# Two transformer blocks on one core: the weight sums of the fast downward products move from SBUF to DRAM

## The reference, cut to what matters

```python
# block 1
f = (jax.nn.silu(h @ w_gate[l]) * (h @ w_up[l])) @ w_down[l]
...
# block 2
def conv_gated_mlp(h, w_up, conv_w, conv_b, w_down):
...
    return (jax.nn.silu(gate) * val) @ w_down
```

## Time and profile before

| | us |
|---|---|
| median of 3 runs | 1310.57 (1309.82 to 1311.11) |
| the profiled execution: its own time | 1310.27 |
| span from its first to its last instruction | 1308.5 |
| PE busy | 1267.4 (97%) |
| DVE, ACT, POOL busy | 966.4 (74%), 730.3 (56%), 559.4 (43%) |

### The profile page before, as it was taken

One profiled execution on the slowest core, in us unless ns is written; L12 is line 12 of the kernel. 1 busy time (PEld: TensorE's weight loads), 2 busy tenths in 40 slices (PEclk: granted clock), 3 DMA queues, 4 the chain that ended last, 5 costly groups with the idle time before them and its releaser, 6 DMA issues. The chain is left out here.

```text
span 1308.5 us, 22029 instructions
## 1 busy us (share of the span) xinstructions
PE 1267.4 (97%) x7684; PEld 1148.4 (88%) x7684; DVE 966.4 (74%) x1732; ACT 730.3 (56%) x1437; POOL 559.4 (43%) x626
## 2 busy tenths in 40 slices
PE   8999999999999977999999999999999999788998
PEld 7999988999999956889999999889899998567887
DVE  5677857899888966785565788377977777858754
ACT  5666745455555535556667788254555554445452
POOL 5655672356565543226777765310213222641000
PEclk9999999999999999999999999999999999998999
DMA  6321213343333399722212333232232323797221
GB/s 194 87 73 58 97 66 97 97 129 97 99 125 97 108 300 233 173 73 74 73 49 65 74 67 112 80 123 91 81 100 94 112 80 113 265 225 191 99 97 65
DMA packets 134855, 148.28 MB, mean 113 GB/s; under 512 B 24652, under 2 KB 110875, under 8 KB 134770
## 3 DMA queue, kind: packets, MB, share of 16 engines
q1 hardware_dynamic: 121536, 126.27, 30.4%
q0 software_dynamic: 13232, 20.89, 8.3%
q10 hardware_dynamic: 2, 0.00, 0.0%
HBM read 132.47 MB, written 2.10 MB: 103 GB/s over the span
## 5 line engine op out<-in xcount | busy, mean ns | idle before, releaser
L2836 PE MATMUL ps<-h_hi,w_hi 128*128 128x256 f32 (+1 forms) x748 | 238.4, 319 | 0.0
L2837 PE MATMUL ps<-h_lo,w_hi 128*128 128x256 f32 (+1 forms) x748 | 237.4, 317 | 0.0
L2838 PE MATMUL ps<-h_hi,w_lo 128*128 128x256 f32 (+1 forms) x748 | 237.1, 317 | 0.0
L2955 PE MATMUL ps<-w_hi,h_hi 128*128 128x384 f32 (+2 forms) x512 | 162.6, 328 | 0.0
L2957 PE MATMUL ps<-w_hi,h_lo 128*128 128x384 f32 (+2 forms) x512 | 157.9, 319 | 0.0
L2836 PEld LDWEIGHTS ps<-h_hi,w_hi 128*128 128x128 f32 x748 | 142.6, 191 | 9.6 <-DVE h_lo L2132 0.3
L2838 PEld LDWEIGHTS ps<-h_hi,w_lo 128*128 128x128 f32 x748 | 142.5, 191 | 9.6
L2837 PEld LDWEIGHTS ps<-h_lo,w_hi 128*128 128x128 f32 x748 | 142.6, 191 | 8.4
L3132 PE MATMUL ps<-w_hi,st_hi 128*128 128x512 f32 x252 | 104.5, 415 | 30.5 <-DVE w_lo L2385 18.1
L1249 POOL TENSOR_TENSOR w_lo<-w_raw,w_hi 128x384 fp32r<-128x384 f32 (+2 forms) x114 | 112.9, 1012 | 34.1 <-ACT w_hi L1512 34.1
L3133 PE MATMUL ps<-w_lo,st_hi 128*128 128x512 f32 x252 | 102.2, 405 | 0.0
(11 more groups left out here) (331 smaller groups left out, 3437.5 us busy)
## 6 DMA issues: line engine op xcount, KB each, us to landing
w_raw<-in_w_up_dram SPq DMA_DIRECT2D x25, 1024.0 KB, 5.3
w_raw<-in_w_in_dram SPq DMA_DIRECT2D x69, 256.0 KB, 3.6
w_raw<-in_w_down_dram SPq DMA_DIRECT2D x14, 1024.0 KB, 6.3
w_raw<-in_w_gate_dram SPq DMA_DIRECT2D x11, 1024.0 KB, 5.3
w_raw<-in_w_out_dram SPq DMA_DIRECT2D x8, 1024.0 KB, 5.0
h_raw<-in_w_down_dram SPq DMA_DIRECT2D x8, 1024.0 KB, 8.1
h_raw<-h_raw POOLq DMA_DIRECT2D x32, 256.0 KB, 5.3
w_raw<-in_w_up_dram SPq DMA_DIRECT2D x16, 512.0 KB, 3.8
```

The costliest lines, as they stand in the source:

```text
L2836: pe.matmul(out_, s_hi, m_hi, start=first and n == 0, stop=False, skip_group_check=True)
L2837: pe.matmul(out_, s_hi, m_lo, start=False, stop=False, skip_group_check=True)
L2838: mm = pe.matmul(out_, s_lo, m_hi, start=False, stop=last and n == len(pairs) - 1, skip_group_check=True)
L2955: pe.matmul(bank, h_hi[:, kb0 + i, tok], hi[:, i, :], start=half == 0 and i == 0, stop=False, skip_group_check=True)
```

## The change

It makes all weight sums ahead of the downward stages, in DRAM. Each block gets a DRAM tensor `down_sums[d]` with room for T1, T4, T2 and T3 of all nine pairs (256 KB each).

* SP's `sums_begin` copies, for each pair, B21 and B22 (512 KB, to T4's and T2's place) and B12 twice (256 KB each, to T1's and T3's place), DRAM to DRAM: 27 transfers a block, one pair after each projection load.
* POOL's `sums_added` issues 12 adding transfers a block, four (T3, T1, T2, T4) for each of three groups of three pairs, 768 KB each. They stand in POOL's mixer work right behind the attention units listed in ADD_AFTER. T2 = T2 + T1 waits for T1 to land (`sums_chain`), T4 waits for T2 in the same way, T3 for the copies (`sums_begun`); T1 has no wait of its own.
* The downward stages have no sums or adding transfers of weights any more. SP loads a quarter from `w_down` and three sums from `down_sums` (256 KB and 768 KB), or 512 KB and one sum of 256 KB. `down_high` on ACT waits for the loads alone. POOL issues the loads of `early_hi` together after part P4 of step 1, and those of `early_lo` together when `early_negated` allows.
* On DVE, in step 10, the block that makes `first_two` and the kept sums now stands ahead of `down_low` of B2 and `rows_added`.

```diff
-SUMMED = 4
+GROUPS = 3
+ADD_AFTER = ((9, 12, 15, 18, 20, 23, 25, 27, 29, 32, 35, 38), (8, 11, 14, 17, 20, 23, 26, 29, 32, 35, 38, 41))
+SUM_T1, SUM_T4, SUM_T2, SUM_T3 = range(4)
...
+        down_sums = [nc.dram_tensor(f"down_sums{d}", [STRASSEN, P, 4, 512], F32, kind="Internal").ap() for d in range(2)]
...
+            def group(g):
+
+                wide = STRASSEN // GROUPS
+                return slice(wide * g, wide * g + wide)
...
+                    if i < STRASSEN and j % (STRASSEN // GROUPS) == 0:
+                        sp.wait_ge(sums_ready[j // (STRASSEN // GROUPS)], 32 * d + 32)
                     if i < STRASSEN:
-                        sp.dma_start(dst.rearrange("p (k h) n -> p k (h n)", k=RB), src).then_inc(done, 16)
+                        sp.dma_start(dst[:, 0, :], src[:, 0, LEFT]).then_inc(done, 16)
+                        sp.dma_start(dst[:, 1:4, :], down_sums[d][j, :, 0:3, :]).then_inc(done, 16)
                     else:
                         sp.dma_start(dst[:, 0:2, :].rearrange("p h n -> p (h n)"), src[:, 1, :]).then_inc(done, 16)
-                        sp.dma_start(dst[:, 2, :], src[:, 0, RIGHT]).then_inc(done, 16)
+                        sp.dma_start(dst[:, 2, :], down_sums[d][j, :, SUM_T3, :]).then_inc(done, 16)
...
+            def sums_begin(d, j):
+
+
+                pair, g = slice(j, j + 1), j // (STRASSEN // GROUPS)
+                w = rows(A[("w_down", "w_down_2")[d]][0])
+                sp.dma_start(down_sums[d][j, :, SUM_T4:SUM_T2 + 1, :].rearrange("p h n -> p (h n)"), w[j][:, 1, :])\
+                    .then_inc(sums_begun[g], 16)
+                for n in (SUM_T1, SUM_T3):
+                    sp.dma_start(down_sums[d][j, :, n, :], w[j][:, 0, RIGHT]).then_inc(sums_begun[g], 16)
...
+                        normed_units += 1
+                        if normed_units in ADD_AFTER[mx.b]:
+                            n = ADD_AFTER[mx.b].index(normed_units)
+                            sums_added(mx.b, n // 4, ("T3", "T1", "T2", "T4")[n % 4])
...
+            def sums_added(d, g, name):
+
+
+                to = lambda n: down_sums[d][group(g), :, n, :]
+                from_w = lambda quarter: weight_quarter(d, group(g), quarter)
+                chain, ready = sums_chain[g], sums_ready[g]
+                if name == "T3":
+                    pool.wait_ge(sums_begun[g], 48 * (STRASSEN // GROUPS) * (d + 1))
+                    pool.dma_start(to(SUM_T3), from_w("B22"), accum_op=ALU.add).then_inc(ready, 16)
+                elif name == "T1":
+                    pool.dma_start(to(SUM_T1), from_w("B11"), accum_op=ALU.add).then_inc(chain, 16)
+                elif name == "T2":
+                    pool.wait_ge(chain, 32 * d + 16)
+                    pool.dma_start(to(SUM_T2), to(SUM_T1), accum_op=ALU.add).then_inc(chain, 16)
                 else:
-                    pool.wait_ge(down_added[n], added_at(d, i, k))
-                pool.dma_start(raw[:, dst, :], raw[:, src, :], accum_op=ALU.add).then_inc(down_added[n], 16)
-
-            def down_additions(d, i):
-
-                for n, k in ((i - 2, 2), (i - 1, 1), (i, 0)):
-                    if SUMMED <= n < STEPS and (n < STRASSEN or k == 0):
-                        down_added_to(d, n, k)
+                    pool.wait_ge(chain, 32 * d + 32)
+                    pool.dma_start(to(SUM_T4), to(SUM_T2), accum_op=ALU.add).then_inc(ready, 16)
...
             def down_high(d, i, name):
 
-                if name in ("B11", "B2"):
-                    act.wait_ge(down_raw[down_place(i)], raw_at(d, i))
-                else:
-                    sem_, value = weight_sum_ready(d, i, SUMS_OF[name])
-                    act.wait_ge(sem_, value)
+                act.wait_ge(down_raw[down_place(i)], raw_at(d, i))
```

More of the change, by code:

```diff
@@ L103, in before_in_place @@
     return earlier[-1] if earlier else None
[L106 to L117, removed]
 def weights_hi_at(d, i, k):
@@ L138, in raw_at @@
     same = [n for n in range(STEPS) if down_place(n) == down_place(i)]
-    return 16 * sum(1 if n < STRASSEN else 2 for e in range(d + 1) for n in same if e < d or n <= i)
+    return 32 * sum(1 for e in range(d + 1) for n in same if e < d or n <= i)
 def round_done(j, k=SEVEN):
@@ L833, in two_blocks_kernel @@
         down_raw = [sem(f"down_raw{n}") for n in range(6)]
-        down_added = [sem(f"down_added{n}") for n in range(6)]
-        down_sums = sem("down_sums")
+        sums_begun = [sem(f"sums_begun{n}") for n in range(GROUPS)]
+        sums_chain = [sem(f"sums_chain{n}") for n in range(GROUPS)]
+        sums_ready = [sem(f"sums_ready{n}") for n in range(GROUPS)]
         down_hi = sem("down_hi")
@@ L1022, in down_raw_of, with weight_quarter @@
             return h_raw[:, n - 2, :, :]
-        def weight_sum_ready(d, i, k):
-            return (down_sums, weight_sums_at(d, i, k)) if i < SUMMED else (down_added[down_place(i)], added_at(d, i, k))
+        def weight_quarter(d, pairs, name):
+            k, h = {"B11": (0, 0), "B12": (0, 1), "B21": (1, 0), "B22": (1, 1)}[name]
+            w = A[("w_down", "w_down_2")[d]][0].rearrange("(j k p) (h n) -> j p k h n", p=P, k=RB, n=512)
+            return w[pairs, :, k, h, :]
+        def group(g):
+            wide = STRASSEN // GROUPS
+            return slice(wide * g, wide * g + wide)
         def down_piece(w, i, name):
@@ L1175, in _ @@
             const(pool_gain[:, :], A["pool_scale"][0].rearrange("(m p) -> p m", p=P), allow_slow_non_contiguous=True)
+            begun = 0
             for n in range(2, len(mixers[0].loads)):
                 load_projection(mixers[0], n)
+                if n >= 3 and begun < STRASSEN:
+                    sums_begin(0, begun)
+                    begun += 1
+            for j in range(begun, STRASSEN):
+                sums_begin(0, j)
             out_chunks(A["w_out"][0], C_OUT1, 0)
@@ L1184, in _ @@
                     load_projection(mixers[1], n)
+                if n >= 2 and begun < STRASSEN:
+                    sums_begin(1, begun)
+                    begun += 1
+            for j in range(begun, STRASSEN):
+                sums_begin(1, j)
             out_chunks(A["w_out_2"][0], C_OUT2, 1)
@@ L1253, in mixer @@
                 own_n, own_d = mx.cnt.of[mx.steps[0]]["N"], 0
+                normed_units = 0
                 for s in mx.orders["pool"]:
@@ L1337, in gate_sums @@
                 pool.tensor_tensor(s3, a11, a21, ALU.subtract).then_inc(gate_w_sums, 1)
[L1339 to L1347, removed]
@@ L1429, in _ @@
                 at_ += wide
[L1430 to L1447, removed]
+            pool.wait_ge(hid_done, MT)
+            pool.wait_ge(down_part, part_at(0, 1, "P4"))
+            for part, src in sources:
+                pool.dma_start(early_hi[:, :, part], src).then_inc(early_high, 16)
+            pool.wait_ge(early_negated, 2)
+            for part, src in sources:
+                pool.dma_start(early_lo[:, :, part], src, accum_op=ALU.add).then_inc(early_low, 16)
             norm(2, True)
@@ L1474, in _ @@
             pool.wait_ge(gate_part, SEVEN * (N_MIXED - 1) + 1)
-            down_sums_of(1, 0)
             first_sums_low("T4", 3)
             first_sums_low("T2", 4).then_inc(first_sums_lo, 1)
[L1478 to L1485, removed]
+            pool.wait_ge(gate_part, SEVEN * N_MIXED)
+            gain(6, gain_pre[:, :], "ln_ple_2")
             norm(4, False)
@@ L2440, in down_steps @@
                                 .then_inc(down_summed, 1)
+                    down_low(d, i, "B2")
+                    if i + 1 < STEPS:
+                        rows_added(d, i + 1)
                     rows_low(d, i, 0)
```

10 lines of the change are left out of this document (1 added, 9 removed).

## The result

The changed kernel takes 1381.3 us (median of 4 runs, 1379.5 to 1383.5) against 1310.8 us for the kernel before in the same sessions: ratio 1.0537, 95% interval 1.0519 to 1.0556. It is slower by 70.5 us. The forecast was 1345, slower, with a range of 1264 to 1390. The direction was right, and so was the place of most of it, the mixers; the loss was twice the 34 us foretold.

What follows compares the result with a forecast made beforehand. PE was taken to bound the kernel, busy 1267.4 of 1308.5 us, with room only in the downward stages. 1310.3 - 44 (downward stages) + 79 (additions in the mixers) = 1345 us, range 1264 to 1390.

Steps and rivals of the forecast that it cites:

- Downward stages, -44: Both downward stages: with weight additions out of the chain, PE's stops for late weights go, gaining 44 us together.
- The two waits at its head: First downward stage: short PE waits for `hid` and `st_lo` of rows would stay, about 3.2 us.
- the count of 63 parts: Downward stages: PE's work without stops taken as 63 parts of 1.36 us, 85.7 us a stage.
- 25.5 us that I called lost: First downward stage before the change: 111.2 us taken against 85.7 us of parts, the rest counted as lost.
- The reordered block, with the tightness 0.6 us lost: DVE's step 10 in the downward stages: shorter way to `first_two`, put with DVE barely keeping up at 0.6 us lost.
- Copies, 0 to 5: 27 DRAM copies a block: cost 0, or up to 5 us if they delay projection loads.
- T1's landing time, 24 us: Mixers: three times `early_lo`'s median, rounded up, for 768 KB, both ends in DRAM and a source in three blocks.
- The forecast's other estimate: T1 in the mixers: 23 to 55 us if only 3 engines share it, 128 rows each.
- POOL's waits with issues and clock, 55 + 4 + 4 + 12 = 75: Mixers: T2's wait on PE's path 55 us, T4's 4, POOL's issues 4, PE's slower clock around six stops 12.
- Held transfers, 4 us: Mixers: projection loads, 3.6 us each and landing shortly before ACT copies them, lose 4 us beside long additions.
- Longer still: Mixers: additions slow each other and projection loads, or T1 takes 34 us; 1405 us, chance 0.10.
- Hidden: Mixers: T1 lands before POOL reaches T2, leaving issues and a clock stop or two; 1269 us, chance 0.32.

Runs made afterwards that it cites:

- the ladder: Changed kernel with work left out: no T2 and T4 1316.6 us, no T1 and T3 1271.2, no additions 1268.4, neither additions nor copies 1266.4.
- e7: Changed kernel with one group of nine pairs instead of three of three, T1 and T3 one 2.3 MB transfer each: 1311.9 us.
- e1: Changed kernel with the patterns of T1 and T3 turned to rows outermost, 128 x 3 x 512 on both sides: 1277.9 us.
- e3: Changed kernel without T2 and T4, so POOL never waits for an addition; T1 and T3 keep their slow pattern: 1316.6 us.
- e5: Changed kernel without its 24 additions, the copies kept, so downward products use unsummed weights: 1268.4 us.
- e6: Changed kernel with slow patterns kept, T2 and T4 issued some ten units behind T1: 1353.7 us.
- e2: Changed kernel with T1's pattern alone turned to rows outermost, T3 still in three blocks: 1369.6 us.

## Why the prediction was half right

**Downward stages, -44: right in size, in part by luck.** 42.0 by the two traces, 44.5 by the ladder. The first stage took 88.3 + 0.68 = 89.0 us for 88.9, but not as replayed. The two waits at its head, put at 3.2 us, are gone: PE has no stop in this stage. In their place stand 24 matmuls of the product ahead of it (L2832 to L2834, 2.9 us), which run between the first parts before and after the change, and which the count of 63 parts had left out. They were part of the 25.5 us that I called lost. The second stage has no such matmuls; it kept 2.5 us more than forecast: the list of waits shows 2.0 where 1.2 were allowed for, and the other 1.7 has no row. That DVE just keeps up held: 5.41 us for a step, 5.3 forecast.

**The reordered block, with the tightness 0.6 us lost: wrong in sign.** Against the old order it gains 3.4 us by the times and 2.5 inside the stages by the traces (88.4 and 88.7 us from first to last start for 89.7 and 89.9). The other 0.9 lies outside them. The view was there: 2.5 us of waiting for `first_two` before:

```profile
PE ps L3132 <- DVE first_two L2435: 2.5, 1, 2.5
```

I took it for a symptom of DVE's general lateness; with the old order PE waits there (3.5 us) even when the stage has no additions in it.

**Copies, 0 to 5: about 2,** as far as two sessions can tell.

**T1's landing time, 24 us: the step was right and its size low.** It measured 28.9. Three times the median of `early_lo` was a fair price, but of its three reasons only the last, the source in three blocks, counts: e7 shows that the bytes hardly matter in this pattern, and e1 that DRAM at both ends does not. The forecast's other estimate, 23 to 55 us from 128 rows on each of three engines, rested on that reason, and I gave it no weight in the sum. The waits at T2 were 103.7 us for 87 forecast; T2 and T4, put at 10 us, took 8.6 and 9.9; T4's waits on POOL were 11.5, of which 4 were to reach PE.

**POOL's waits with issues and clock, 55 + 4 + 4 + 12 = 75: 64.7 measured** (1381.3 - 1316.6). By stretches outside the downward stages PE's idle time is 95.7 us in the changed kernel and 41.3 in e3, 54.4 apart, and its busy time 1021.9 and 1010.9, 11.0 apart, which is the slower clock. So 11 for 12 for the clock, and 54 for 63 for the rest. That this is so near is partly luck: with T1 at 28.9 the same sum asks for 6 x 28.9 - 56.9 - 32.2 = 84 us of waits on PE's path instead of 55. One reason for the difference is seen in the traces: stops overlap, since PE already stands for a held load when POOL waits.

**Held transfers, 4 us: this is the step that failed.** The ladder gives 1316.6 - 1268.4 = 48.2 us. By the same stretches e3 has 33.7 us more idle time of PE than e5, and 13.5 more busy time, the slower clock (47.2 together in these two profiles). I had seen that projection loads land 1 to 2 us before ACT needs them, and named the case under *Longer still*, but priced a load beside a long addition by the mean share of the DMA engines, as late by a fraction of its 3.6 us. A round of them was complete up to 22.7 us after its last issue, 19 late. A mean share of 0.24 says nothing of the few engines that carry a slow transfer: every load has a share on those engines as well, and the counts show just these shares late.

In sum: 75 + 4 = 79 was forecast and 64.7 + 48.2 = 112.9 measured. With the copies and the downward stages that is 112.9 + 2.0 - 44.5 = 70.4, the 70.5 measured to 0.1. The prices go by taking things out in this order; another order might share them out in another way. The rival *Hidden* needed T1 within its distance, at 6 to 12 us, and e1 is that case: 1277.9 us for 1269 forecast.

## What to carry to other kernels

Before a transfer is made bigger by taking several blocks at once, look at the order of its dimensions: rows outermost, blocks within, on both sides, landed in 8.9 us here where blocks outermost took 28.9. A slow transfer is dearer than the wait for it: check what shares its queue and its engines (48 us here, with nobody waiting for the transfer itself), and mend all slow ones, since one left over holds what is issued behind it. An engine's wait that shows no releaser may be a load; compare the moment of its end with the landings. Where several transfers in flight count up one semaphore, trust only the landing of the last.

## What the runs showed that was not expected

* A fast transfer issued behind a slow one in POOL's queue lands 4 to 6 us after it: T2 in 24.0 to 27.5 us instead of 8.5 (e6), T1 in 25.9 instead of 8.9 (e2). A table landed in 19.8 us, 0.6 us after the slow one.
* SP's loads are held too, though SP has its own queue: a round of three is complete after up to 22.7 us instead of 3.6, with nine of the round's 48 counts late, three for each load. SP's own issuing of a load then takes up to 6.2 us instead of 0.5. Why the issuing slows down, these runs don't tell.
* The rows of one block set the time of an addition in blocks of rows, and not the bytes: 768 KB in three blocks of 128 rows 28.9 us, 2.3 MB in nine such blocks 28.4. Blocks of another height were not tried.
